# Seven of the eight rounds of an MLP's down projection by Strassen's seven block products

## The reference, cut to what matters

```python
hm = rms_norm(x, norm_mlp)
x = x + jnp.square(jax.nn.relu(hm @ w_up)) @ w_down     # w_up 1024 x 4096, w_down 4096 x 1024
y = rms_norm(x, norm_final)                             # prompt and sample tokens
```

## Time and profile before

| what | value |
|---|---|
| median of 3 runs | 2284.49 us (2283.61 to 2286.02) |
| the profiled execution, its own time | 2284.73 us |
| its span, first to last instruction | 2282.9 us |
| mean granted TensorE clock | 0.999 |
| busy in the span: PE / DVE / ACT / POOL | 99% / 40% / 24% / 37% |

### The profile page before, as it was taken

One profiled execution on the slowest core, in us unless ns is written; L12 is line 12 of the kernel. 1 busy time (PEld: TensorE's weight loads), 2 busy tenths in 40 slices (PEclk: granted clock), 3 DMA queues, 4 the chain that ended last, 5 costly groups with the idle time before them and its releaser, 6 DMA issues. The chain is left out here.

```text
span 2282.9 us, 33306 instructions
## 1 busy us (share of the span) xinstructions
PE 2258.6 (99%) x13404; PEld 2140.3 (94%) x13404; DVE 902.9 (40%) x1439; ACT 555.6 (24%) x923; POOL 842.0 (37%) x888
## 2 busy tenths in 40 slices
PE   8999999999999999999999999999999999999998
PEld 7999999999999999999999999888989889899896
DVE  5589865445543442101212114443242332423324
ACT  4333231111232222121121212232212112121132
POOL 4677543333222224242242425323324233242351
PEclk9999999999999999999999999999999999999999
DMA  4111221121222332212112122211111111111112
GB/s 149 52 54 50 70 86 38 40 59 58 58 58 78 86 117 67 86 38 86 47 47 86 40 83 86 65 38 47 45 44 41 46 46 46 46 38 45 46 56 79
DMA packets 168152, 139.53 MB, mean 61 GB/s; under 512 B 5794, under 2 KB 146422, under 8 KB 168027
## 3 DMA queue, kind: packets, MB, share of 16 engines
q1 hardware_dynamic: 165405, 127.83, 19.2%
q0 software_dynamic: 2304, 8.91, 1.0%
q10 hardware_dynamic: 326, 1.12, 0.1%
HBM read 119.47 MB, written 18.73 MB: 61 GB/s over the span
## 5 line engine op out<-in xcount | busy, mean ns | idle before, releaser
L736 PE MATMUL acc<-h_hi,w_hi 128*128 128x368 f32 (+1 forms) x2584 | 851.5, 330 | 1.7 <-POOL w_lo L1512 1.1
L738 PE MATMUL acc<-h_hi,w_lo 128*128 128x368 f32 (+1 forms) x2584 | 845.2, 327 | 0.0
L737 PE MATMUL acc<-h_lo,w_hi 128*128 128x368 f32 (+1 forms) x2584 | 844.3, 327 | 0.0
L1512 POOL TENSOR_TENSOR w_lo<-w_raw,w_hi 128x256 fp32r<-128x256 f32 (+1 forms) x491 | 467.2, 978 | 840.6 <-ACT w_hi L1160 840.6
L736 PEld LDWEIGHTS acc<-h_hi,w_hi 128*128 128x128 f32 x2584 | 485.4, 188 | 7.3 <-issue 4.0
L737 PEld LDWEIGHTS acc<-h_lo,w_hi 128*128 128x128 f32 x2584 | 485.4, 188 | 0.3
L738 PEld LDWEIGHTS acc<-h_hi,w_lo 128*128 128x128 f32 x2584 | 485.3, 188 | 0.0
L1160 ACT ACTIVATE w_hi<-w_raw 128x1024 fp32r<-128x1024 f32 (+1 forms) x169 | 176.3, 1044 | 497.2 <-PE acc L738 444.4
L1787 DVE TENSOR_TENSOR x<-acc,x 128x512 f32<-128x512 f32 (+1 forms) x291 | 201.0, 691 | 180.9 <-PE acc L738 173.0
L736 PE MATMUL acc<-w_hi,u_hi 128*128 128x512 f32 x480 | 187.2, 390 | 0.9 <-POOL w_lo L1512 0.9
L737 PE MATMUL acc<-w_lo,u_hi 128*128 128x512 f32 x480 | 187.1, 390 | 0.0
(11 more groups left out here) (394 smaller groups left out, 2700.1 us busy)
## 6 DMA issues: line engine op xcount, KB each, us to landing
w_raw<-in_w_in SPq DMA_DIRECT2D x84, 512.0 KB, 3.9
w_raw<-in_w_up SPq DMA_DIRECT2D x32, 512.0 KB, 4.0
w_raw<-in_w_down SPq DMA_DIRECT2D x32, 512.0 KB, 3.7
b_raw<-branch_outputs POOLq DMA_DIRECT2D x16, 544.0 KB, 6.2
w_raw<-in_w_branch SPq DMA_DIRECT2D x16, 512.0 KB, 3.5
xin<-in_x_prompt SPq DMA_DIRECT2D x8, 512.0 KB, 7.8
x<-in_x_prompt SPq DMA_DIRECT2D x16, 256.0 KB, 5.3
w_raw<-in_w_out SPq DMA_DIRECT2D x8, 512.0 KB, 3.7
```

The lines of the kernel that those rows point to most:

```text
L736: pe.matmul(out, lh, rh, start=first, stop=False)
L737: pe.matmul(out, lh, rl, start=False, stop=False)
L738: return pe.matmul(out, ll, rh, start=False, stop=last)
L1512: return pool.tensor_tensor(out, x, y, op)
```

## The change

The down projection of rounds 0 to 6 is cut into blocks: the 1024 prompt tokens into two halves, the 512 hidden features of the round into two halves (feature blocks 0 and 2, and 1 and 3, which `q` counts), the 1024 output columns into two halves. Instead of the eight block products (token half x feature half x column half) it makes seven products of sums of blocks, in the form with shared sums, as seven stages `st`. A stage has 4 token tiles (`p` = 0 to 3) of 2 x 3 matmuls of 512 columns. The sample tile (`p` = 4) is still done by its plain four block products of 4 matmuls, in stages 0, 1, 4 and 5.

- The seven left operands (two 256-feature slices each of 512 tokens by 128) are A11, A21, A12, A22 straight from relu and square, and four sums that DVE makes (`a_first`, `a_others`); ACT makes their high, POOL their low halves (`a_split`, `a_rest`).
- The seven right operands are four blocks of `w_down` as loaded and three sums (stages 1, 3, 6), whose making (`down_sums`) and low halves (`down_low`) are DVE's; ACT makes all seven high halves, POOL the other four low halves (`down_lo`).
- Weights go through a ring of three buffers with 11 operands a round (4 up, 7 down). A high half may be made when PE has left the operand three before (`op_end`).
- Partial sums that several output blocks share stay in the five banks `pz` and in `acc` over stages; DVE adds the bank of each of the 32 groups of a round to `x1` (33 additions of 512 columns, 36 before).
- `w_down` is loaded in rows of 1024 columns. POOL's low halves are cut into pieces of 256 columns. The loops over rounds are written out. The load of the final norm's gain moves from before round 0 to the last round. Some semaphores of the norms are merged under one name.

The core of the diff (merged semaphore names, placement of buffers in memory and the last round's renamed helpers are left out):

```diff
...
-L_UN, L_BN, L_GN, L_IT = 8, 16, 48, 8
+L_UN, L_BN, L_GN, L_IT = 4, 4, 44, 8
...
+DOWN = [(0, p) for p in (0, 1, 2, 3, 4)] + [(1, p) for p in (0, 1, 4, 2, 3)] + [(2, p) for p in range(4)] + \
+    [(3, p) for p in range(4)] + [(4, p) for p in (4, 0, 1, 2, 3)] + [(5, p) for p in (0, 1, 4, 2, 3)] + \
+    [(6, p) for p in range(4)]
...
+SAMPLES = {0: (0, 0), 1: (0, 1), 4: (2, 1), 5: (1, 0)}
+A_READY = (9, 11, 12, 13, 14, 15, 16)
+U_ORDER = ([0, 1, 2, 3, 4, 5, 6, 7], [0, 1, 7, 2, 3, 4, 5, 6])
...
+def down_bank(st, p):
+    if p == 4 or (p == 3 and st in (1, 6)):
+        return "pz", 4
+    return ("acc", p) if st in (1, 6) else ("pz", p)
+def targets(st, p):
+    if p == 4:
+        return [(NT, SAMPLES[st][1])]
+    if st == 1:
+        return [(4 + p, 1), (4 + p, 0)] if p == 3 else [(4 + p, 1)]
+    return [{0: (p, 0), 2: (4 + p, 0), 3: (4 + p, 1), 4: (p, 1), 5: (p, 0), 6: (4 + p, 0)}[st]]
...
+        w_sum = sb(top, "w_sum", [P, SLOTS, UNIT])
...
+            w_c = sb(st, "w_c", [P, 3, 512], F32R)
+            a_op = sb(st, "a_op", [P, 2, 2, 7, 512], F32R)
+            f0_raw = sb(st, "f0_raw", [P, 2, UNIT])
...
+            a_raw = sb(st, "a_raw", [P, 2, 2, 7, 512])
+        f1_raw = w_raw
...
+        def slot(n):
+            return n % 3 if n < 11 * END else (n - 11 * END) % 2
...
+        def op_end(n):
+            n -= 3 if n < 11 * END else 2
+            if n < 0:
+                return {-2: L_G, -1: L_G + 3}[n]
+            i, j = n // 11, n % 11
+            return L_G + i * L_GN + (3 * j + 3 if j < 4 else 12 + STAGE_END[j - 4])
...
+        def u_parts(s, g):
+            q, one, two = s // 2, *((0, 3) if s % 2 == 0 else (5, 6))
+            first, second = a_sums(q, one), a_sums(q, two)
+            return [[(first[:, 0:368], 0, 368)],
+                    [(first[:, 368:512], 0, 144), (second[:, 0:224], 144, 368)],
+                    [(second[:, 224:512], 0, 288), (packs_raw[:, q, s % 2, TS:], 288, 352)]][g]
...
+            def up_load(i, s):
+                u = L_U + i * L_UN + s
+                sp.wait_ge(w_ready, u - SLOTS + 1)
+                if i and s < 2:
+                    sp.wait_ge(sem("d_lo"), 4 * i)
+                    sp.wait_ge(sem("d_sums"), 8 * i)
+                f = i * 512 + s * P
+                sp.dma_start(raw(u, KT), a["w_up"][0, :, f:f + P].rearrange("(k p) n -> p k n", p=P)) \
+                    .then_inc(w_loaded[u % SLOTS], 16)
+            def down_load(i):
+                if i == 0:
+                    sp.wait_ge(group_ready, L_G + 3)
+                for q in range(2):
+                    f = i * 512 + q * 256
+                    sp.dma_start(f0_raw[:, q, :], w_down[f:f + P, :]).then_inc(sem("f0_in"), 16)
+                for q in range(2):
+                    f = i * 512 + q * 256 + P
+                    sp.wait_ge(w_ready, L_U + i * L_UN + 3 + (L_U + q) % 2)
+                    sp.dma_start(f1_raw[:, q, :], w_down[f:f + P, :]).then_inc(sem("f1_in"), 16)
+            for i in range(END):
                 for s in range(4):
-                    loop_load(L_U, i, L_UN, s, raw(L_U + s, KT), up(s))
-                for s in range(4):
-                    loop_load(L_U, i, L_UN, 4 + s, raw(L_U + s, 2), down(s))
-
-            with sp.Fori(0, END) as i:
-                mlp_loads(i, lambda s: a["w_up"][0, :, bass.ds(i * 512 + s * P, P)].rearrange("(k p) n -> p k n", p=P),
-                          lambda s: w_down[bass.ds(i * 512 + (s // 2) * 256, 256), (s % 2) * 512:(s % 2 + 1) * 512]
-                          .rearrange("(k p) n -> p k n", p=P))
-            mlp_loads(END, lambda s: a["w_up"][0, :, END * 512 + s * P:END * 512 + (s + 1) * P]
-                      .rearrange("(k p) n -> p k n", p=P),
-                      lambda s: w_down[END * 512 + (s // 2) * 256:END * 512 + (s // 2 + 1) * 256,
-                                       (s % 2) * 512:(s % 2 + 1) * 512].rearrange("(k p) n -> p k n", p=P))
+                    up_load(i, s)
+                down_load(i)
...
+            def down(i):
+                stage = None
+                last = {("pz", b): (i - 1, max(e for e, d in enumerate(DOWN) if down_bank(*d) == ("pz", b)))
+                        for b in range(5)}
+                for e, (st, p) in enumerate(DOWN):
+                    if st != stage:
+                        stage = st
+                        if st in (1, 3, 6):
+                            pe.wait_ge(sem("d_lo_v"), 3 * i + (1, 3, 6).index(st) + 1)
+                        else:
+                            pe.wait_ge(sem("d_lo"), 4 * i + (0, 2, 4, 5).index(st) + 1)
+                        pe.wait_ge(sem("u_ready"), 16 * i + A_READY[st])
+                    b = down_bank(st, p)
+                    if b in last:
+                        if last[b][0] >= 0:
+                            pe.wait_ge(sem("l_added"), 32 * last[b][0] + last[b][1] + 1)
+                    else:
+                        pe.wait_ge(acc_free[b[1]], L_B + 4 + i * L_BN)
+                    last[b] = (i, e)
+                    out = (pz if b[0] == "pz" else acc)[:, b[1], :]
+                    _, hi, lo = ring(11 * i + 4 + st)
+                    if p == 4:
+                        if st == 0:
+                            pe.wait_ge(sem("u_ready"), 16 * i + 11)
+                        both = packs[:, :, SAMPLES[st][0], :]
+                        pe.matmul(out, both[:, 0, :], hi[0], start=True, stop=False)
+                        pe.matmul(out[0:TS], both[:, 0, 0:TS], lo[0], start=False, stop=False)
+                        pe.matmul(out[0:TS], both[:, 1, 0:TS], lo[1], start=False, stop=False)
+                        mm = pe.matmul(out, both[:, 1, :], hi[1], start=False, stop=True)
+                    else:
+                        new = st in (0, 1, 5) or (st == 6 and p == 3)
+                        for q in range(2):
+                            mm = product(out, a_hi(q, st)[:, p * P:p * P + P], a_lo(q, st)[:, p * P:p * P + P],
+                                         hi[q], lo[q], new and q == 0, q == 1, not new)
+                    mm.then_inc(group_ready, 1)
...
+            for i in range(END):
+                if i == 0:
+                    up_hi(0, 1)
+                else:
+                    up_hi(i, 2)
+                for g in range(3):
+                    relu_in(i, 0, g)
+                if i == 0:
+                    up_hi(0, 2)
+                up_hi(i, 3)
+                for g in range(3):
+                    relu_in(i, 1, g)
+                down_hi(i, 0)
+                relu_in(i, 2, 0)
+                a_split(i, 0, U_ORDER[0][:4])
+                relu_in(i, 2, 1)
+                a_split(i, 0, U_ORDER[0][4:])
+                relu_in(i, 2, 2)
+                down_hi(i, 1)
+                relu_in(i, 3, 0)
+                a_split(i, 1, U_ORDER[1][:1])
+                relu_in(i, 3, 1)
+                relu_in(i, 3, 2)
+                a_split(i, 1, U_ORDER[1][1:3])
+                down_hi(i, 2)
+                a_split(i, 1, U_ORDER[1][3:4])
+                down_hi(i, 3)
+                a_split(i, 1, U_ORDER[1][4:6])
+                down_hi(i, 4)
+                a_split(i, 1, U_ORDER[1][6:])
+                down_hi(i, 5)
+                down_hi(i, 6)
+                up_hi(i + 1, 0)
+                if i + 1 < END:
+                    up_hi(i + 1, 1)
...
+            def a_rest(i, q, some):
+                for j in some:
+                    pool.wait_ge(sem("u_high"), 16 * i + 8 * q + U_ORDER[q].index(j) + 1)
+                    pool.wait_ge(sem("a_sums"), 10 * i + (5 if q == 0 else 6 if j == 0 else 10))
+                    if j == 7:
+                        ins = tt(packs[:, q, :, TS:], packs_raw[:, q, :, TS:],
+                                 packs[:, q, :, 0:TS].bitcast(F32), ALU.subtract)
+                    else:
+                        for c0 in (0, 256):
+                            c = slice(c0, c0 + 256)
+                            ins = tt(a_lo(q, j)[:, c], a_sums(q, j)[:, c], a_hi(q, j)[:, c].bitcast(F32),
+                                     ALU.subtract)
+                    ins.then_inc(sem("u_ready"), 1)
+            for i in range(END):
+                if i == 0:
+                    up_lo(0, 1)
+                up_lo(i, 2)
+                up_lo(i, 3)
+                down_lo(i, 0)
+                a_rest(i, 0, U_ORDER[0])
+                down_lo(i, 1)
+                a_rest(i, 1, U_ORDER[1][:3])
+                down_lo(i, 2)
+                a_rest(i, 1, U_ORDER[1][3:4])
+                down_lo(i, 3)
+                a_rest(i, 1, U_ORDER[1][4:6])
+                down_lo(i, 4)
+                a_rest(i, 1, U_ORDER[1][6:])
+                down_lo(i, 5)
+                down_lo(i, 6)
+                up_lo(i + 1, 0)
+                if i + 1 < END:
+                    up_lo(i + 1, 1)
...
+            def a_first(i, q):
+                dve.wait_ge(acc_free[2], L_B + i * L_BN + 2 * q + 1)
```

(68 more changed lines are left out.)

318 lines of the change are left out of this document (196 added, 122 removed).

## The result

The median of the changed kernel is 2256.59 us (2256.06 to 2256.90, four runs), that of the kernel before in the same session 2284.66 (2283.61 to 2286.02, four runs): 28.1 us less, a ratio of 0.9877 with the interval 0.9859 to 0.9894. I forecast 2255.5. A repeat in another session gave 0.9876 (0.9861 to 0.9891).

The account below looks back on a forecast made before the run. TensorE bounds the kernel, at work in 99% of the span, so time is matmuls times their distance. Saving 5.44 less 1.3 us of wait gives 4.14 a round, 29.0 in seven: 2255.5 us, range 2246 to 2267.

Parts of the forecast that it names:

- The matmuls removed: Down part, rounds 0 to 6: 24 fewer 512-column matmuls at 0.2267 us save 5.44 us a round, 38.1 in seven.
- The wait: PE at stage 0's sample tile waits for POOL's low half of the packed samples; 1.3 us a round, restart included.
- the chain: Relu, squares, `a_others`, ACT copy, POOL pieces, counted from D, when PE finishes the up part; PE asks at D+5.44.
- The collision: Behind the up part, `down_low(1)` on DVE slows POOL's pieces for the samples; adds 0.4 us to PE's wait.
- Two of the signs: Signs of the forecast: PE waiting 1.0 to 1.5 us a round, and POOL's pieces beside `down_low(1)` over 1 us.
- The cover of stage 0, "only about one microsecond thick": Before stage 0: first part of q=1 ready at D-1.1, D being when PE finishes the up part; cost nothing.
- No wait at all: Rival: POOL gets its turn first and hand-overs are shorter, so PE never waits for the samples; 2246.4 us, chance 0.17.
- Stage 0 begins late too, and both waits add: Rival: cover used up and samples' wait longer, 1 to 2 us more a round; 2262 to 2270 us, chance 0.17.
- The clock falls at each wait: Rival: two microseconds a round at 1.2 GHz behind the wait add 7 us in all; 2262 us, chance 0.04.
- Slower than before: Rival: DVE holds off POOL's 17 pieces before stage 0, 1.5 us each instead of 0.71; 2340 us, chance 0.03.
- The next thing late, at most 0.3 us (stage 1's last tile): DVE reads sample bank `pz` 4 by D+12.3, PE wants it at D+12.4; 0 in the sum, 0.3 in the range.
- Transfers, unrolling, POOL's and DVE's totals at nothing: Weight loads land in time, written-out loops cost PE nothing, DVE's 44 and POOL's 43 us a round set no pace.

Follow-up runs that it names:

- Experiment 4: Changed kernel with stage 5's products made twice, so 24 product matmuls of 512 columns come back each round; 2295.51 us.
- experiment 2: Changed kernel with DVE making stage 1's low halves (`down_low(1)`) before the last up group instead of behind its sums; 2254.99 us, ratio 0.9865 to the kernel before.
- experiment 6: Changed kernel with four extra POOL pieces of 256 columns a round, into an unused tile, before the parts of slice q=1; 2257.45 us.
- experiment 3: Changed kernel with POOL instead of DVE making the three weight sums' low halves, in pieces of 256 columns; 2255.23 us, ratio 0.9867 to the kernel before.
- experiment 1: Changed kernel with POOL making the packed samples' low half before part 1 in slice q=1; 2251.41 us, ratio 0.9849 to the kernel before.
- experiment 7: Changed kernel with eight extra POOL pieces of 256 columns a round, into an unused tile, before the parts of slice q=1; 2290.26 us.
- experiment 5: Changed kernel with both edits: samples' low half before part 1, and `down_low(1)` before the last up group; 2249.11 us, ratio 0.9843 to the kernel before.
- experiment 8: Changed kernel with the ring's second operand of three, not its third, in the added buffer (`w_c`, `w_d`); 2255.84 us.
- experiment 9: Changed kernel with a small tile placed ahead so that `w_d` begins at a multiple of 64 bytes; 2257.53 us.

## Why the prediction was right, point by point

- **The matmuls removed** (24 x 0.2267 = 5.44 us a round): right. Experiment 4 put them back: 38.3 us by the trace for 168 (37.6 by the times), where the step had 38.1.
- **The wait**: right in its place and its number, and near in its size, 1.24 us against the plan and 1.15 against a round without it, where I had 1.3. Link by link the chain ran 0.04 to 0.07 us ahead of the forecast, and POOL was done at D+6.47 instead of D+6.6. The collision was 0.34 instead of 0.4 us, and experiment 2 removed it. The restart, read from the earlier trace rows as 0.15, was 0.16 to the first start (6.60 less 5.46 for the products and 0.98 idle), and 0.07 more in the four behind it. Two of the signs that I had named came out short all the same: PE is idle for 0.90 to 0.99 us, not 1.0 to 1.5, and POOL's pieces beside `down_low(1)` take 0.88 us each, not over 1.
- **The cover of stage 0, "only about one microsecond thick"**: the step that was mis-sized. In the changed kernel POOL is done with the first part of q=1 at 1740.47 + 1.42 = 1741.89, 2.9 us before D, and experiment 6 found 2.8. POOL's work on q=0, and DVE's five sums beside it:
```profile
1727.89 11.60 POOL L1724 TENSOR_TENSOR a_op<-a_raw,a_op 128x256 fp32r<-128x256 f32 x14 [0.82 <-ACT a_op L1308]
```
```profile
1734.33 1.13 DVE L2046 TENSOR_TENSOR a_raw<-a_raw 128x512 f32<-128x512 f32 x1
1735.38 2.37 DVE L2046 TENSOR_TENSOR w_sum<-f_raw,w_raw 128x512 f32<-128x512 f32 x2
1737.67 2.37 DVE L2046 TENSOR_TENSOR f_raw<-f_raw,w_sum 128x512 f32<-128x512 f32 x2
```
I had stacked two pessimistic terms. The sums of q=0 were ready at D-17.7, 1.6 us late by the forecast's own count and not 2.5. From D-16.9 on POOL took 12.6 us for its pieces of q=0 until the first of q=1, where I had 10.6 and 3.0 for DVE's five sums: they cost POOL 2.0 us. The row where two such operations cost 0.43 would have given 1.1, too little. And DVE paid more than POOL did, 5.7 us for five operations that I had at 3.0. (The forecast's D-16.8 and 10.6 us make D-6.2; the D-5.5 there leaves 0.7 us in between, which it does not name; the trace has 0.7 us there too, for ACT's first copy.)
- **No wait at all** (2246.4): this rival needed the chain to be shorter by a microsecond. The order of two parts on POOL does nearly that: with both edits the time is 2249.11, PE doesn't wait, and 2.7 us stay against 2246.4. The seven down parts have 295.0 us where 7 x 41.8 = 292.6 was planned; that is the longer distances, of which the kernel before had 0.1 a round too.
- **Stage 0 begins late too, and both waits add** (2262 to 2270): wrong in its mechanism, not only in its odds. In experiment 3 a round pays one of the two waits, in experiment 6 it pays both and no more in sum than the one. Had the cover been gone by up to a microsecond, the time would hardly have changed.
- **The clock falls at each wait** (2262): not at these waits. Behind 0.90 us the starts are 0.31, 0.22 and 0.24 apart at a clock of 1.00, so the swing that the Trainium skill describes (TensorE: Matmul & The Clock Gate, "A second HAM failure mode: psum-queue depth-cycling") is not seen at them. But its chance was not to be had from the length of the gap alone. Earlier in the program, outside the change, PE is idle for 0.94 us ahead of 18 small matmuls. In the trace of the changed kernel the clock stays at 1.00 behind them; in that of experiment 1 it falls to 0.50, and 368-column matmuls come 0.31 us apart:
```profile
345.77 2.00 PE L1000 MATMUL pz<-proj_a 128*128 128x64 f32 x16 [0.94 <-DVE proj_a L2046]
```
```profile
349.00:350.00 1.00, 1.00 (x5) 1.00 (x4) 1.00 (x2) 0.00 (x0) 0.19 (x1) 0.50 0.83 220
```
What decides it no run here shows. Behind 4.25 us it fell in all seven rounds of experiment 7, at 1.6 us a round.
- **Slower than before** (2340, from a delay of POOL of 5.2 us on, less 1.1 of cover, so with PE 4.1 us late): no such delay. Experiment 7 made PE 4.4 us late and ended at 2290.26, 5.6 us slower than before. The rival had added the samples' wait, which falls away, and left out the start at half clock. With 1.6 us for that and 0.3 for the longer distances it decides once PE is 5.44 - 0.3 - 1.6 = 3.5 us late, an estimate, if a gap of that length already lowers the clock, which no run here shows.
- **The next thing late, at most 0.3 us (stage 1's last tile)**: not in the changed kernel, since PE's wait for the samples gives DVE its time. In experiment 1, with that wait gone, it came in two rounds of seven, 0.5 us each. It was the right place.
- **Transfers, unrolling, POOL's and DVE's totals at nothing**: right; no other wait stands in PE's list. DVE has 47.8 us a round where I had 44, POOL 49.7 where I had 43.
- **Not foreseen**: the distance in some stages, 0.2304 us (5.53 / 24) instead of 0.2267. Without any wait (experiment 5) a down part takes 42.1 us on average, 0.3 more than the kernel before less its 24 matmuls (47.3 - 5.44); the up parts add a few hundredths. So the forecast was too low by 0.33 us a round for this and too high by 0.15 for the wait. The two errors partly cancel, and what is left, 0.2 a round, is the 1.1 us by which the forecast was low.

Experiments 4 and 6 to 9 have one timed run each; their verdicts rest on the trace. So do the gains of some 2 us in experiments 2 and 3. Not tried: taking the link through ACT out of the samples' chain, and other places for the ring than these.

## What to carry to other kernels

Where one engine is at work for 99% of the time, price what you take from it by the distance of its starts, then follow each serial chain that the new order hangs on a moment of that engine, hand-over by hand-over: the chain cost 1.15 us of the 5.44 while its engines were idle for 45% of the round or more. Swapping two entries of an order took most of it away, and moving two operations took the rest. Two waits behind one another on the same engine don't add if the second one's producer isn't moved by the first; forecast the later of the two deadlines, not their sum. The gaps of 0.9 us here cost their length and some 0.2 us; those of 4.3 us also cost a start at half the clock.

## What the hardware showed that was not expected

- The same matmul of 512 columns comes every 0.2267 us or every 0.2304 us, depending on which of three places its moving operand lies in; the effect moved with the place (experiment 8), and moving `w_d` to a multiple of 64 bytes did not change it (experiment 9).
- Behind an idle gap of 4.25 us, seven matmuls ran at the 1.2 GHz level, 0.43 us apart; behind the seven waits of 0.9 us none did. Behind the same gap of 0.94 us and 18 small matmuls at 346 us the clock fell in one execution (experiment 1) and not in another (the changed kernel).
- DVE and POOL slow each other down, both ways: POOL's two pieces rose from 1.42 to 1.76 us beside a DVE pair (experiment 2), and the DVE pair from 1.29 to 1.70 us where POOL began 0.56 us into it (experiment 1). Beside POOL's unbroken pieces, five DVE sums took 5.7 us, and one alone took 4.47 us while POOL lost nothing (experiment 3).
